# Two mixing layers: keys, queries, values and the scan's head norm in one stage, and the span sums of the chunk loop earlier

## The reference, cut to what matters

```python
h = _rmsnorm(x, mix_norm[l]); proj = h @ w_in[l]
c_q, c_kv, k_pe, hq, hf, hi, hg = jnp.split(proj, splits, axis=-1)
# _mla: 4 heads, 128 plain and 64 rotary dimensions, latent ranks 384 (queries) and 256 (keys, values)
q = (_rmsnorm(c_q, q_a_norm) @ w_q_b).reshape(B, S, 4, 192); q_nope, q_pe = q[..., :128], q[..., 128:]
q_pe = _apply_rope(q_pe, cos, sin); k_pe = _apply_rope(k_pe, cos, sin)     # one k_pe for all heads
kv = (_rmsnorm(c_kv, kv_a_norm) @ w_kv_b).reshape(B, S, 4, 256); k_nope, v = kv[..., :128], kv[..., 128:]
s = einsum(q_nope * scale, k_nope) + einsum(q_pe * scale, k_pe); p = softmax(masked s); a = einsum(p, v)
# _hgrn2: 4 heads of 128, chunks of 64: o from a decayed scan, then
r = _rmsnorm(o, out_norm) * silu(g_raw)
x = x + jnp.concatenate([a, r], axis=-1) @ w_out[l]
```

## Time and profile before

| | us |
|---|---|
| median of the runs, lowest, highest | 6319.23, 6315.79, 6324.01 |
| the profiled execution's own time, its span | 6303.05, 6301.4 |
| busy PE, PEld, DVE, ACT, POOL | 5405.9, 4596.0, 2798.3, 2172.3, 364.6 |
| share of the span of PE, DVE, ACT | 86%, 44%, 34% |
| mean granted clock of TensorE, as a share of the full one | 0.915 |

### The profile page before, as it was taken

The page is one execution under the profiler, slowest core; times in us unless marked ns, Lnnn a source line. Parts: engine busy times, 40 slices in busy tenths (PEclk is TensorE's granted clock), DMA queues, the critical chain, the costliest instruction groups (busy, mean ns, idle before and its releaser), DMA issues. The chain is left out here.

```text
span 6301.4 us, 97705 instructions
## 1 busy us (share of the span) xinstructions
PE 5405.9 (86%) x38244; PEld 4596.0 (73%) x38245; DVE 2798.3 (44%) x4351; ACT 2172.3 (34%) x3192; POOL 364.6 (6%) x574
## 2 busy tenths in 40 slices
PE   6964876869888969999798797599999999999994
PEld 5653774657764659999676456598989889898994
DVE  2695332542462345555317233344444445454444
ACT  2212113532333334444333232233333444444432
POOL 0111000000140000000004000100000000000001
PEclk8985997979989979999899888699999999999997
DMA  2110001031000165555210004544444445545544
GB/s 78 39 48 2 2 4 71 0 117 50 24 5 12 54 245 209 197 194 202 85 39 5 17 0 176 179 159 157 157 158 159 174 180 188 185 180 186 185 159 170
DMA packets 110153, 701.23 MB, mean 111 GB/s; under 512 B 12736, under 2 KB 16592, under 8 KB 68560
## 3 DMA queue, kind: packets, MB, share of 16 engines
q1 hardware_dynamic: 95920, 651.24, 28.6%
q0 software_dynamic: 9184, 28.49, 1.3%
q10 hardware_dynamic: 4800, 17.83, 0.7%
HBM read 633.13 MB, written 64.38 MB: 111 GB/s over the span
## 5 line engine op out<-in xcount | busy, mean ns | idle before, releaser
L3075 DVE TENSOR_TENSOR experts_low<-experts_raw,experts_high 128x1024 fp32r<-128x1024 f32 x678 | 810.7, 1224 | 1022.3 <-ACT experts_high L3004 1022.3
L2939 PE MATMUL ps<-experts_xs_high,experts_high 128*128 128x256 f32 (+1 forms) x3584 | 1038.6, 290 | 52.3 <-issue 51.2
L2939 PE MATMUL ps<-experts_xs_low,experts_high 128*128 128x256 f32 (+1 forms) x3584 | 1039.7, 290 | 0.0
L2939 PE MATMUL ps<-experts_xs_high,experts_low 128*128 128x256 f32 (+1 forms) x3584 | 1039.4, 290 | 0.0
L2939 PEld LDWEIGHTS ps<-experts_xs_high,experts_high 128*128 128x128 f32 x3584 | 682.8, 191 | 64.9 <-issue 55.5
L3004 ACT ACTIVATE experts_high<-experts_raw 128x1024 fp32r<-128x1024 f32 x678 | 687.7, 1049 | 63.4 <-DMA experts_raw<-experts 63.4
L2939 PEld LDWEIGHTS ps<-experts_xs_low,experts_high 128*128 128x128 f32 x3584 | 680.3, 190 | 9.4
L2939 PEld LDWEIGHTS ps<-experts_xs_high,experts_low 128*128 128x128 f32 x3584 | 681.2, 190 | 0.0
L2623 PE MATMUL ps<-dense_xs_parts,dense_high 128*128 128x256 f32 x2816 | 499.1, 280 | 4.0 <-DVE dense_xs_parts L2726 2.7
L2623 PEld LDWEIGHTS ps<-dense_xs_parts,dense_high 128*128 128x128 f32 x2816 | 436.5, 189 | 12.3 <-issue 4.8
L2931 PE MATMUL ps<-experts_high,experts_hid_high 128*128 128x512 f32 x1120 | 444.6, 397 | 0.0
(11 more groups left out here) (530 smaller groups left out, 9262.5 us busy)
## 6 DMA issues: line engine op xcount, KB each, us to landing
experts_raw<-experts SPq DMA_DIRECT2D x226, 1536.0 KB, 6.2
dense_raw<-dense SPq DMA_DIRECT2D x90, 1536.0 KB, 6.7
mixT<-w_in SPq DMA_DIRECT2D x36, 512.0 KB, 3.6
y_slot<-route_blank SPq DMA_DIRECT2D x15, 1152.0 KB, 19.2
out_proj_raw<-w_out SPq DMA_DIRECT2D x48, 256.0 KB, 2.7
proj_keys_raw<-w_in SPq DMA_DIRECT2D x20, 512.0 KB, 3.6
x_mixed<-x_out SPq DMA_DIRECT2D x16, 512.0 KB, 4.7
y_slot<-experts_y ACTq DMA_DIRECT2D x8, 1024.0 KB, 9.2
```

Source lines behind the costliest of these rows:

```text
L2939: last = nc.tensor.matmul(ps[:, m, 0:width], w[:, u, m, c], x[:, k, 0:width], start=(k == 0 and i == 0), stop=(k == KD - 1 and i == 2))
L3075: nc.vector.tensor_tensor(low[:, v, t, :], raw[:, v % NR, t, :], high[:, v, t, :].bitcast(F32), ALU.subtract).then_inc(split, 1)
```

## The change

The six stages become two: one new function `lift_and_norm` and the attention. The order of `behind` in the chunk loop changes. `head_norm_gate` and `rotate` are deleted; `gemm_t` and `product_rows` stay for other callers. In `lift_and_norm`:

- All products of keys, queries and values are in two parts (three fp32r products each). The five blocks of the input `down` are split once.
- Twelve units (4 of keys, 8 of queries) pass through three pairs of PSUM banks; weights in two buffers; banks 6 and 7 serve the rotary key, the sums and the turned norms.
- The norm's sums stand behind units 4 to 7, its turns behind units 9, 10, 11 and value block 3. Its sums of four heads are inverted together.
- The rotary queries are multiplied by the table on the way out of PSUM (VectorE) and stay 128 rows; the rotary key is folded by a "fold" of 128 columns, so its 128 rows hold the sum twice. The scores' rotary product has 128 rows and adds the halves.
- Values are read out by ScalarE instead of VectorE.

```diff
-                  ("earlier", 128), ("iota8", 8), ("tok", 8), ("pass", NPASS + 1), ("fold", 64), ("spans", 512)):
+                  ("earlier", 128), ("iota8", 8), ("tok", 8), ("pass", NPASS + 1), ("fold", 128), ("spans", 512)):
+def lift_and_norm(core, name, w_q, w_k, w_v, down, queries, keys, values, key_rope, table, oT, gain, gated, sq):
+    units = [(w_k[n], (3, 4)) for n in range(4)] + [(w_q[n], (0, 1, 2)) for n in range(8)]
+    order = (3, 4, 0, 1, 2)
...
+        def _(sp):
+            for n in range(U):
+                if n >= 2:
+                    sp.wait_ge(split, n - 1)
+                sp.dma_start(raw[:, n % 2, 0:size(n)], units[n][0]).then_inc(loaded[n % 2], 16)
+                if n == 3:
+                    sp.dma_start(raw_v[:, :, :], w_v.rearrange("(k p) n -> p k n", p=P)).then_inc(loaded_v, 16)
...
+        def _(pe):
+            def turn(j):
+                pe.wait_ge(spreaded, j + 1)
+                if j >= 1:
+                    pe.wait_ge(normed, j)
...
+            for n, (_, blocks) in enumerate(units):
+                pe.wait_ge(split, n + 1)
+                pe.wait_ge(x_split, 2 if n < 4 else 5)
+                if 3 <= n < 11:
+                    pe.wait_ge(freed_a, n - 2)
+                elif n >= 11:
+                    pe.wait_ge(freed_d, n - 10)
+                for k, c in enumerate(blocks):
+                    w = slice(k * P, (k + 1) * P)
+                    for j, (a, x) in enumerate(((high, x_high[:, c, :]), (high, x_low[c]), (low, x_high[:, c, :]))):
+                        for h in range(2):
+                            last = nc.tensor.matmul(core.ps[:, 2 * (n % 3) + h, :], a[:, n % 2, w], x[:, h * HALF:(h + 1) * HALF], ...
+                if n == 1:
+                    pe.wait_ge(key_scaled, 1)
+                    ... 2 products with core.c("fold") into banks 6, 7
+                if 4 <= n < 8:
+                    ... 8 products of 128x1 with core.c("ones"), head n - 4
+                if n >= 9:
+                    turn(n - 9)
+            pe.wait_ge(v_split, 2)
+            for b in range(NT):
+                ... 6 products of 128x512 into bank b % 6
+                if b == 3:
+                    turn(3)
...
+        def _(act):
+            round_unit(0)
+            for m, c in enumerate(order):
+                copy(x_high[:, c, :], down[:, c, :], ACT.Copy).then_inc(x_rounded, 1)
+                if m == 1:
+                    round_unit(1)
+            for n in range(U):
+                if n + 2 < U:
+                    round_unit(n + 2)
+                if n < 8:
+                    act.wait_ge(product, n + 1)
+                    copy(keys[:, n, :] if n < 4 else queries[:, n - 4, :], two(2 * (n % 3)), ACT.Copy).then_inc(freed_a, 1)
+                if n == 2: ... key_rope read out
+                if 2 <= n < 6: ... square of head n - 2
+                if n in (6, 7): ... values' weights rounded
+                if n == 8: ... root, then spread heads 0 and 1;  n in (9, 10): spread heads 2, 3
+            for b in range(NT):
+                act.wait_ge(v_made, b + 1)
+                copy(values[:, b, :], core.ps[:, b % 6, :], ACT.Copy).then_inc(v_placed, 1)
...
+        def _(dve):
+            split_unit(0)
+            for m, c in enumerate(order):
+                dve.wait_ge(x_rounded, m + 1)
+                tt(x_low[c], down[:, c, :], x_high[:, c, :].bitcast(F32), ALU.subtract).then_inc(x_split, 1)
+                if m == 1:
+                    split_unit(1)
+            tt(down[:, 5, :], down[:, 5, :], table[:, :], ALU.mult).then_inc(key_scaled, 1)
+            for n in range(U):
+                ... split_unit(n + 2); gate times head at n 1 to 4; reciprocal at n 8
+                if n >= 10:
+                    norm(n - 10)
+                if n >= 8:
+                    dve.wait_ge(product, n + 1)
+                    tt(rope[:, n - 8, :], two(2 * (n % 3)), table[:, :], ALU.mult).then_inc(freed_d, 1)
+            norm(2)
+            norm(3)
@@ gated_chunks, TensorE, behind
                 last.then_inc(s["turned"], 1)
+                if sums:
+                    ahead(n + 2, u, i + 1)
                 pe.wait_ge(s["k_rows"], n + 1)
...
                     mm(ps[:, 7, h * P:(h + 1) * P], kt[:, h % 2, :], value[:, u, h * P:(h + 1) * P], start=True, stop=True)
-                if sums:
-                    ahead(n + 2, u, i + 1)
                 pe.wait_ge(s["attn_ready"], n + 1)
@@ mix_layer
-            gemm_t(core, f"up_q{l}", d[f"w_q{l}"], 8, 3, down, lambda n: at(queries, n))
-            rotate(core, f"rotate{l}", [queries[:, 4 + j, :] for j in range(4)] + [down[:, 5, :]], table, turned)
-            gemm_t(core, f"up_k{l}", d[f"w_k{l}"], 4, 2, down[:, 3:5], lambda n: at(keys, n))
-            product_rows(core, f"up_v{l}", down[:, 3:5, :], 2, d[f"w_v{l}"], 1, values)
+            lift_and_norm(core, f"lift{l}", d[f"w_q{l}"], d[f"w_k{l}"], d[f"w_v{l}"], down, queries, keys, values, key_rope[:, :], table,
+                          z, core.v(f"hgn{l}", 0), mixT[:, 4:8, :], mixT[:, 0:4, :])
```

More of the change, by code:

```diff
@@ L633, in rwkv_chunks @@
     halves = (slice(0, 64), slice(64, 128))
-    fold = core.c("fold")
+    fold = core.c("fold")[:, 0:64]
     later = lambda n, k: not isinstance(n, int) or n >= k
@@ L1689, in _ @@
         @block.vector
         def _(dve):
[L1691 to L1710, removed]
+            tt = nc.vector.tensor_tensor
+            def split_unit(n):
+                dve.wait_ge(rounded, n + 1)
+                part = (slice(None), n % 2, slice(0, size(n)))
+                tt(low[part], raw[part], high[part].bitcast(F32), ALU.subtract).then_inc(split, 1)
@@ new lines, in norm @@
+            def norm(j):
+                dve.wait_ge(turned, j + 1)
+                dve.wait_ge(gated_done, j + 1)
+                nc.vector.scalar_tensor_tensor(gated[:, j, :], gated[:, j, :], gain, two(6), ALU.mult, ALU.mult).then_inc(normed, 1)
+            split_unit(0)
[4 more added lines that the diff above has]
+                    split_unit(1)
@@ new lines, in _ @@
+            tt(down[:, 5, :], down[:, 5, :], table[:, :], ALU.mult).then_inc(key_scaled, 1)
+            for n in range(U):
+                if n + 2 < U:
+                    split_unit(n + 2)
+                if 1 <= n < 5:
+                    tt(gated[:, n - 1, :], gated[:, n - 1, :], oT[:, n - 1, :], ALU.mult).then_inc(gated_done, 1)
+                if n in (6, 7):
+                    dve.wait_ge(v_rounded, n - 5)
+                    tt(low_v[:, n - 6, :], raw_v[:, n - 6, :], high_v[:, n - 6, :].bitcast(F32), ALU.subtract).then_inc(v_split, 1)
+                if n == 8:
+                    dve.wait_ge(sums, 4)
+                    nc.vector.tensor_scalar(stat[:, 0, :], core.ps[:, 6, 0:4 * NT], 1.0 / P, 1e-6, ALU.mult, ALU.add).then_inc(meansq, 1)
+                    dve.wait_ge(rooted, 1)
+                    nc.vector.reciprocal(stat[:, 2, :], stat[:, 1, :]).then_inc(inverse, 1)
+                if n >= 10:
[3 more added lines that the diff above has]
+                    tt(rope[:, n - 8, :], two(2 * (n % 3)), table[:, :], ALU.mult).then_inc(freed_d, 1)
@@ L2233, in _ @@
             advance(NCH - 1, 1, NCH // 2 - 1)
[L2234 to L2302, removed]
@@ L3205, in mix_layer @@
         down = sb("down", [P, 6, T])
+        z = sb("z", [P, 4, T])
         with ExitStack() as s2:
             sb2 = lambda name, shape: s2.enter_context(nc.sbuf_tensor(f"{name}{l}", shape, F32))
-            z = sb2("z", [P, 4, T])
             qk = sb2("qk", [P, 2, 4, T])
@@ L3223, in mix_layer @@
             gated_chunks(core, f"gated{l}", qk, log_decays, inputs, z)
-            head_norm_gate(core, f"gated_norm{l}", z[:, :, :], core.v(f"hgn{l}", 0), mixT[:, 4:8, :])
         with ExitStack() as s2:
             sb2 = lambda name, shape: s2.enter_context(nc.sbuf_tensor(f"{name}{l}", shape, F32))
-            turned = sb2("turned", [64, 5, T])
             values = sb2("values", [P, NT, HALF])
-            queries = sb2("queries", [P, 8, T])
-            nope = queries[:, 0:4, :]
+            queries = sb2("queries", [P, 4, T])
             keys = sb2("keys", [P, 4, T])
-            gemm_t(core, f"up_q{l}", d[f"w_q{l}"], 8, 3, down, lambda n: at(queries, n))
-            rotate(core, f"rotate{l}", [queries[:, 4 + j, :] for j in range(4)] + [down[:, 5, :]], table, turned)
-            gemm_t(core, f"up_k{l}", d[f"w_k{l}"], 4, 2, down[:, 3:5], lambda n: at(keys, n))
-            product_rows(core, f"up_v{l}", down[:, 3:5, :], 2, d[f"w_v{l}"], 1, values)
-            qbuf = down[:, 0:2, :]
-            vbuf = down[:, 2:4, :].rearrange("p u (b n) -> p u b n", b=NT)
-            rbuf = down[0:64, 4:6, :]
+            key_rope = sb2("key_rope", [P, T])
+            lift_and_norm(core, f"lift{l}", d[f"w_q{l}"], d[f"w_k{l}"], d[f"w_v{l}"], down, queries, keys, values, key_rope[:, :], table,
+                          z, core.v(f"hgn{l}", 0), mixT[:, 4:8, :], mixT[:, 0:4, :])
```

(9 more changed lines are left out.)

79 lines of the change are left out of this document (77 added, 2 removed).

## The result

The changed kernel takes 6127.72 us (median of 4 runs, 6119.84 to 6131.06), the kernel before beside it 6317.51 (4 runs, 6312.17 to 6324.01): a ratio of 0.9697, 95% interval 0.9681 to 0.9714. That is 189.8 us less. The recorded execution took 6131.06 us with a span of 6129.4, so the spans of the two recorded executions differ by 172.0 us.

| | before, layers 0 and 1 | after | change | forecast |
|---|---|---|---|---|
| chunk loop, first level product to last z | 128.7, 127.5 | 117.0, 116.9 | -22.3 | -21.6 |
| from there to mla's first product | 132.7, 136.6 | 83.6, 83.7 | -102.0 | -101.2 |
| mla, first product to out_proj's first load | 147.0, 159.5 | 124.9, 124.8 | -56.8 | -17.5 |
| all else | | | +9.1 | 0 |

A forecast was written before the change was run, and what follows sets the result against it. TensorE, busy 86% of the span, was taken to hide one-engine-at-a-time chains in the stages before the attention. Gains of 101.2 (merged stage), 21.6 (chunk loop) and 17.5 (attention) sum to 140.3: 6319.23 to 6179 us, range 6150 to 6212.

The forecast's parts named there:

- The merged stage: Six stages from last chunk to attention become one of 76.9 us, against 125.5 and 129.5: 101.2 us less together.
- The chunk loop: Sums placed before the state's products hide the wait for the turned keys' copy, 0.77 us in 28 chunks: 21.6 us less.
- The attention: Mla's halves, all 128 rows, spend 9.2 us at half clock each: 17.5 us less; bounds 25.9 less to 23 more.
- A: Mla: attention does not change, the clock's late rise having nothing to do with 64 rows; 6196 us, chance 0.26.
- B: Merged stage: each of 8 groups of sums drops the clock, 3.0 us lost each, 24 in all; 6203 us, chance 0.16.
- C: Chunk loop: keeps its period, waiting for VectorE's reduction instead of the copy, no gain; 6201 us, chance 0.09.
- D: Merged stage: half clock throughout, 142.1 us a stage, attention's gain gone too; slower than before, 6327 us, chance 0.03.

The follow-up runs named there:

- the grouped run: Changed kernel with scores' rotary product over its first 64 rows, and both 128-row products before both 64-row ones in scores wider than 512 columns: 6412.33 us.

## Why the prediction was wrong

**The merged stage: right.** The first product came at 5.97 us (6.0 predicted), half clock lasted only for the first 5 us of products, the clock was 1.00 in every window of 5 us between 1841 and 1901, and the stage took 76.3 us in all (76.9). The gain was 102.0 us against 101.2.

**The chunk loop: right in its mechanism, and near in its size in part by luck.** It was 22.3 us against 21.6. The wait for the copy went, and the wait for VectorE's reduction appears for only 1.3 us a layer. But a chunk without a new wait saves 1.00 us and not 0.77, and alone the edit gives 28.0. The 5.7 us between 22.3 and 28.0 went mostly to waits for VectorE: TensorE's level products wait 1.1 and 2.6 us for its factors (L2364), which the prediction did not list, against 0.2 and 0.3 in the run with this edit alone, and the reduction takes 2.6 in both layers against 1.8. The clock accounts for about 1 us more: 10.2 us at half clock in the two loops against 8.2. This looks like scatter between executions and not like the merged kernel: in the six runs made from the kernel after, none of which changes this loop, it takes 114.1 to 117.7 us, against 117.0 and 116.9 here and 114.0 and 114.3 for the edit alone.

**The attention: the step that failed** is "No instruction goes: the rotary product keeps its columns. But the clock bears on it." It priced a product by its columns and left only the clock, 17.5 us. Measured: 56.8. Of that, 30.9 is the price of changing between 64 and 128 rows, a term that the prediction put at nothing. Mla has 48 rotary products a layer, 96 changes; 30.9 / 192 = 0.16 each, near the 0.2 of the grouped run and of the timeline. It could have been read before: the weight loads of the kernel before (shown above) stand with 0.76 us of "issue" ahead of them, and each starts with its product. Had the changes of row count cost nothing, the time would have been about 6159 (6127.7 + 30.9), inside the range.

The other 25.9 is clock, and here the term was too small: the two halves of each layer in the changed kernel stood at half clock for 4.0 and 6.8 us, near the first block's attention, and not for 9.2. That 25.9 is also the bound that the prediction worked out, and did not take, is in part luck, since the time at half clock with 64 rows wanders. It is 73.2 us in both layers together before, 93.1 with the chunk edit alone, 69.5 in the changed kernel with 64 rows. Against the changed kernel's 21.5 that is 25.9, 35.8 and 24.0 us of clock. What is left of the difference in mla is the same each time, 30.9, 30.5 and 31.0 us, so the price of the changes does not hang on that wandering.

The Trainium skill ("TensorE: Matmul & The Clock Gate", section "Step-by-step: what each phase is for") says that TensorE "pulls LDWEIGHTS ahead of in-flight MATMULs" when the row groups don't conflict or the load goes to the background buffer, and that the row count doesn't matter for a load's time. The trace agrees on the load's time and puts a limit to the first: in mla of the kernel before the median load of 64 rows takes 0.186 us and that of 128 rows 0.192, but between products of different row counts it was not pulled ahead (0.01 us ahead, and not 0.43); whether the rule's condition on row groups is the cause, no run here shows.

**The rivals.** A (attention unchanged) is false; undoing the rows alone gives the 27.5 us a layer back. B did not occur, and the run with 32 sums in a row shows its mechanism at 4.1 to 4.4 us a layer. C and D are false. A price for the change of row count was not among the rivals, and so the range's lower end was too high.

**The remainder.** All else together took 9.1 us more in the trace. 8.6 of it shows at the passes of the experts' loop, where TensorE stands before the first product with nothing to wait for. The same group of lines, before, after and with the attention written out (mean ns of one, then idle before):
```profile
L2939 PE MATMUL ps<-experts_xs_high,experts_high 128*128 128x256 f32 (+1 forms) x3584 | 1038.6, 290 | 52.3 <-issue 51.2
```
```profile
L3025 PE MATMUL ps<-experts_xs_high,experts_high 128*128 128x256 f32 (+1 forms) x3584 | 1040.5, 290 | 60.9 <-issue 59.8
```
```profile
L2998 PE MATMUL ps<-experts_xs_high,experts_high 128*128 128x256 f32 (+1 forms) x3584 | 1038.3, 290 | 31.5 <-issue 31.1
```
The medians differ by 189.8 us where the recorded executions differ by 172.0; these 17.8 us of the surprise are the choice of execution. So the 49.5 us between forecast and result are 39.3 from the attention, 1.5 from the merged stage and the chunk loop, 17.8 from the choice of execution, less the 9.1.

## What to carry to other kernels

Do not price a product by its columns alone: look whether its row count differs from its neighbours', and whether the weight load in front of it starts ahead of it or with it. Padding a 64-row product to 128 rows, at equal columns, took 54 us out of two attentions. Where TensorE comes cold to each pass of a loop with copies at its head, try writing the loop out: here it took another 33 us off the same two attentions and the gaps in front of them.

## What was not expected of the hardware

- Changing between stationary tiles of 64 and of 128 rows cost 0.2 us a change at full clock (1.05 against 0.86 us between float32 products of 128x512). Why the load is not pulled ahead there is open.
- With large 64-row products mla stood at half clock for 23 to 51 us a layer (35 in both layers of the two runs made from the changed kernel), with 128-row ones for 11 to 13, with the same changes of size but 64-row products of one column only for 14 and 18. Why the four halves of the kernel before differ so much among each other (9.2 to 29.4 us) stays open.
- The clock fell to 0.50 while TensorE was busy without a gap, behind 32 products of one column.
- The idle time of TensorE at the head of an expert pass, up to 10.3 us, was 49 to 67 us in all in the kernels with looped attention and 31 in the two with it written out, though the experts' code is the same. Nothing was tried on it; its cause is open.
